# Splitting the token axis of a projection's products as 512 and 128 instead of 320 and 320

## What is computed

```python
def conformer_conv_branch(glu_in, conv_buf, w_dw, b_dw, ln_g, ln_b, w_pw):
    u = glu_in[..., :D_CONV] * jax.nn.sigmoid(glu_in[..., D_CONV:])
    v, new_buf = causal_depthwise_conv(u, conv_buf, w_dw, b_dw)
    v = jax.nn.silu(layer_norm(v, ln_g, ln_b))
    return v @ w_pw, new_buf
...
        gates = jax.nn.sigmoid(gate_logits.astype(jnp.float32))
        g_a, g_b = gates[..., :D_MODEL], gates[..., D_MODEL:]
        merged = (g_a * y_a.astype(jnp.float32) + g_b * y_b.astype(jnp.float32)).astype(x.dtype)
        x = x + merged @ p['w_out'][l]
```

## Time and profile before

| | us |
|---|---|
| time, median of 2 runs | 1771.34 |
| the two runs | 1770.57, 1772.12 |
| profiled execution: span, first to last instruction | 1769.8 |
| profiled execution: its own whole time | not listed apart; the two runs are 0.8 and 2.3 above its span |
| TensorE busy in the span | 1729.8 (98%) |
| VectorE busy | 1282.0 (72%) |
| ScalarE busy | 873.9 (49%) |
| mean granted TensorE clock | 0.995 of full speed |

### The profile page before, as it was taken

One profiled execution on the slowest core, in us unless ns is written; L12 is line 12 of the kernel. 1 busy time (PEld: TensorE's weight loads), 2 busy tenths in 40 slices (PEclk: granted clock), 3 DMA queues, 4 the chain that ended last, 5 costly groups with the idle time before them and its releaser, 6 DMA issues.

```text
span 1769.8 us, 29064 instructions
## 1 busy us (share of the span) xinstructions
PE 1729.8 (98%) x11823; PEld 1685.3 (95%) x11823; DVE 1282.0 (72%) x1630; ACT 873.9 (49%) x1491; POOL 116.5 (7%) x173
## 2 busy tenths in 40 slices
PE   7999999999999999999999999999999999999997
PEld 7999999999988999899899989999999999999997
DVE  6864783575757989889898987875547936863865
ACT  5431442243588567747756772274335423431443
POOL 0000000000011011030222102000100000000000
PEclk9999999999999999999999999999999999999998
DMA  4222212213253255183446517212422222212212
GB/s 165 84 72 96 75 69 84 107 49 122 81 172 93 77 168 139 59 227 119 108 126 178 155 49 184 84 61 83 139 84 84 72 69 99 86 61 94 96 63 69
DMA packets 54324, 181.50 MB, mean 103 GB/s; under 512 B 7312, under 2 KB 9520, under 8 KB 49840
## 3 DMA queue, kind: packets, MB, share of 16 engines
q1 hardware_dynamic: 40176, 137.41, 23.7%
q0 software_dynamic: 14016, 42.24, 9.1%
HBM read 155.56 MB, written 16.20 MB: 97 GB/s over the span
## 4 chain that ended last, share of the span: by engine, by line
PE 80%; DVE 11%; ACT 4%; issue 3%; DMA 1%; DVEq 0%; ACTq 0%; SPq 0%
PE ps L1754 30%; PE ps L1862 23%; PE ps L1762 15%; PE ps L1779 4%; PE ps L1815 2%; DVE w_lo L1069 1%; DVE v L1467 1%; DVE acc L1081 1%; PE ps L1797 1%; PE ps L2000 1%; PE ps L1987 1%; ACT w_hi L559 1%; DVE z L1565 1%; DVE y L1616 1%; PE ps L1994 1%
## 5 line engine op out<-in xcount | busy, mean ns | idle before, releaser
L1754 PE MATMUL ps<-xa_hi,w_hi 128*128 128x320 f32 x1328 | 312.9, 317 | 0.1
L1754 PE MATMUL ps<-xa_lo,w_hi 128*128 128x320 f32 x1328 | 302.8, 309 | 0.0
L1862 PE MATMUL ps<-t_hi,w_hi 128*128 128x320 f32 x952 | 295.3, 310 | 6.6 <-DVE sq L1136 5.4
L559 ACT CAST w_hi<-w_raw 128x1024 fp32r<-128x1024 f32 (+2 forms) x183 | 174.6, 955 | 252.2 <-PE ps L1762 174.1
L1862 PE MATMUL ps<-t_hi,w_lo 128*128 128x320 f32 x952 | 294.8, 310 | 0.0
L1862 PE MATMUL ps<-t_lo,w_hi 128*128 128x320 f32 x952 | 294.8, 310 | 0.0
L1069 DVE TENSOR_TENSOR w_lo<-w_raw,w_hi 128x1024 fp32r<-128x1024 f32 (+2 forms) x183 | 203.4, 1112 | 91.5 <-ACT w_hi L559 84.2
L1754 PEld LDWEIGHTS ps<-xa_hi,w_hi 128*128 128x128 f32 x1328 | 222.3, 188 | 12.2 <-issue 10.6
L1467 DVE SCALAR_TENSOR_TENSOR v<-ext_a,par,v 128x640 f32<-128x640 f32 x240 | 211.5, 881 | 15.3 <-ACT v L791 5.8
L1754 PEld LDWEIGHTS ps<-xa_lo,w_hi 128*128 128x128 f32 x1328 | 222.6, 188 | 0.0
L1762 PE MATMUL ps<-xa_hi,w_lo 128*128 128x320 f32 x1328 | 211.7, 310 | 0.0
(11 more groups left out here) (329 smaller groups left out, 2995.5 us busy)
## 6 DMA issues: line engine op xcount, KB each, us to landing
w_raw<-in_w_mix SPq DMA_DIRECT2D x56, 512.0 KB, 3.8
raw_b<-in_w_sp SPq DMA_DIRECT2D x18, 1024.0 KB, 5.0
w_raw<-in_w_sp SPq DMA_DIRECT2D x16, 1024.0 KB, 4.8
w_raw<-in_w_down SPq DMA_DIRECT2D x32, 512.0 KB, 3.7
w_raw<-in_w_tail SPq DMA_DIRECT2D x32, 512.0 KB, 3.7
w_raw<-in_w_gu SPq DMA_DIRECT2D x20, 512.0 KB, 3.8
acb<-cum_dram POOLq DMA_DIRECT2D x20, 512.0 KB, 6.6
w_raw<-in_w_ssm SPq DMA_DIRECT2D x32, 256.0 KB, 2.9
```

What stands on the lines that cost most here:

```text
L559: nc.scalar.copy(hi, w_raw[:, b, 0:width]).then_inc(hi_done, 1)
L1754: nc.tensor.matmul(psj[:, b, u, 0:TH], hi[:, cols], act_in[:, k, u * TH:(u + 1) * TH], start=(k == 0 and n == 0), stop=False)
L1862: last = nc.tensor.matmul(ps[:, sp_set(n) + BANK[q], 0:TH], w[:, k * P:(k + 1) * P], t[:, X_OF[q], k * TH:(k + 1) * TH], start=(first and ...
```

## The change

The jobs of the output projection go through a new function, `job_by_splits`. It cuts the 640 tokens at 512: one product takes tokens 0 to 511, the other 512 to 639. The accumulator of a job is the same pair of banks, now read as one run of 1024 floats of which the first 640 are used: the first product fills the first bank, the second one takes 128 floats of the second. VectorE reads the run of 640 in one piece (`run_out`), where it read two of 320. All 8 jobs run by parts, the first too: it waits for the hi weights at its start, for `ln_lo` ahead of each chunk, and for the lo weights only behind the eighth chunk.

```diff
+        def run_out(b):
+            return psj[:, b].rearrange("p u n -> p (u n)")[:, 0:T]
...
-                nc.vector.tensor_tensor(halved(prod[:]), job_out(b), halved(gate_a[:, c]), ALU.mult).then_inc(evac_done[b], 1)
+                nc.vector.tensor_tensor(prod[:], run_out(b), gate_a[:, c], ALU.mult).then_inc(evac_done[b], 1)
...
+            def job_by_splits(half, b, chunks, in_hi, in_lo, before=None):
+
+                pe.wait_ge(hi_done, 2 * half + b + 1)
+                pe.wait_ge(evac_done[b], half + 1)
+                hi, lo = job_weights(half, b)
+                out = psj[:, b].rearrange("p u n -> p (u n)")
+                parts = (slice(0, 512), slice(512, T))
+                for k in range(chunks):
+                    if before:
+                        before(k)
+                    cols = slice(k * P, (k + 1) * P)
+                    for n, act_in in enumerate((in_hi, in_lo)):
+                        for part in parts:
+                            nc.tensor.matmul(out[:, part], hi[:, cols], act_in[:, k, part],
+                                             start=(k == 0 and n == 0), stop=False)
+                pe.wait_ge(lo_done, 2 * half + b + 3)
+                for k in range(chunks):
+                    cols = slice(k * P, (k + 1) * P)
+                    for part in parts:
+                        last = nc.tensor.matmul(out[:, part], lo[:, cols], in_hi[:, k, part],
+                                                start=False, stop=(k == chunks - 1))
+                last.then_inc(job_done, 1)
...
-            job(half, 0, KM, ln_hi, ln_lo, lambda k: pe.wait_ge(xlo_ready, S_LN + k + 1))
-            job(half, 1, KM, ln_hi, ln_lo)
+            job_by_splits(half, 0, KM, ln_hi, ln_lo, lambda k: pe.wait_ge(xlo_ready, S_LN + k + 1))
+            job_by_splits(half, 1, KM, ln_hi, ln_lo)
             for j in range(1, KM // 2):
                 for b in range(2):
-                    job(half + j, b, KM, ln_hi, ln_lo)
+                    job_by_splits(half + j, b, KM, ln_hi, ln_lo)
```

## The result

The changed kernel takes 1782.99 us (median of two runs, 1781.98 and 1784.01) against 1771.34, 11.6 us slower. The ratio on record is 1.0061, interval 1.0042 to 1.0079 (the two medians alone give 1.0066). In a later comparison with more runs (5 of the changed kernel, 17 of the one before) it took 1782.63 against 1771.68, a ratio of 1.0062, interval 1.0050 to 1.0074. The profiled execution took 1784.01, with a span of 1782.0.

What follows compares the result with a forecast made beforehand. The prediction took PE to bound the kernel, busy 98% of the span. Later jobs +7.6 and first job +1.6 us gave +9.2: span 1769.8 to 1779.0, plus 1.5 for the median, 1780.5 us; range 1774 to 1803.

Steps and rivals of the forecast that it cites:

- The pair: Output projection on PE: one long plus one short product take 338.7 ns, 45.3 more than before; chance 0.69.
- The value taken from products of 64 columns of another data type: Weight load of 112 ns, read from plain f32 products with 128x128 weights, taken as the short product's time.
- 53 (load hidden): Short product's lower bound, 53.3 ns of columns alone; rival with loads hidden, both forms, chance 0.10.
- 227 (plain f32 rate): Short product's upper bound, 226.7 ns at a quarter rate; rival total +29.8 us, 1801, chance 0.18.
- the 13.4 ns: Time per 320-column product beyond its 133.3 ns of columns; taken as fixed, giving the long product 226.7 ns.
- its other candidate: Long product's extra time goes with the columns: 234.7 ns, pair 346.7, total +10.6 us (1781.9).
- The Trainium skill's price: Sustained 81 ns per 128-column and 131 per 512-column product, loads included; 192 pairs would save 15.6 us (1755.7).
- Seven later jobs: Projection jobs after the first, 24 pairs each: 168 x 45.3 ns = +7.6 us, all on the path.
- The first job: Projection's first job: a 1.61 us stall goes, a 2.29 us wait for lo input comes; ends 1.57 us later.
- What was to cost nothing: Accumulator read as one run of 640 (0.824 us either way), weight loads and splits, work of DVE, ScalarE and queues.
- The pair that would make the kernel 2% slower: Pair of some 490 ns (185 ns more), or a new stall, needed for over 2% slower; chance 0.03.
- the clock falling behind a wait of 2.3 us: Half clock after the first job's lo-input wait, 1.6 us lost; given a third, outside the sum.

Runs made afterwards that it cites:

- long products with half loads: Changed kernel, but the 512-token products load 64 weight columns instead of 128, save the first and last of each accumulation; 1771.56 us in one run.
- 448 and 192: Changed kernel with the tokens cut at 448 instead of 512, the accumulator run beginning 64 floats later; 1775.94 us, ratio 1.0025.
- 384 and 256: Changed kernel with the tokens cut at 384 instead of 512, the accumulator run beginning 128 floats later; 1772.30 us, ratio 1.0004.
- the order alone: Kernel before with 320 and 320 tokens kept, only the projection's first job going by parts; 1773.93 us against 1771.47, ratio 1.0013.
- the split alone: Changed kernel with its first job chunk by chunk behind the lo weights, as before the change; 1780.68 us against 1771.47, ratio 1.0053.

## Why the prediction was right

**The pair.** Predicted 338.7 ns, measured 340, by the mechanism that was predicted: the short product lasts as long as the load for the next long one. That the two agree to 1 ns is in part luck, because the two terms were off in opposite directions: 112 and 226.7 predicted, 109 and 231 by the starts of the loads. These starts, to the ns (medians over the seven later jobs), give the time of a product of every width that was run:

| columns | where | measured, ns | columns at 2.4 GHz + 13.4 | columns x 146.7 / 320 |
|---|---|---|---|---|
| 128, next load halved | long products with half loads | 57 | 66.7 | 58.7 |
| 128 | changed kernel | 109 | 66.7 | 58.7 |
| 192 | 448 and 192 | 108 | 93.4 | 88.0 |
| 256 | 384 and 256 | 117 | 120.1 | 117.3 |
| 320 | kernel before | 147 | 146.7 | 146.7 |
| 384 | 384 and 256 | 176 | 173.4 | 176.0 |
| 448 | 448 and 192 | 205 | 200.1 | 205.3 |
| 512 | changed kernel | 231 | 226.7 | 234.7 |

The load's time, 108 to 109 ns, holds behind 128 and 192 columns; a product of 256 columns takes longer by itself and hides it. The value taken from products of 64 columns of another data type carried over to within 4 ns. Of the bounds for the short product, 53 (load hidden) and 227 (plain f32 rate) are both far off.

The prediction took the 13.4 ns as a fixed price per product, and this choice is not borne out: from 128 to 448 columns the times without a wait go with the columns to within 2 ns (last column of the table), which was its other candidate (234.7 for the long product). At 512 columns the measured 231 lies between the two, and why it does is not shown.

**The Trainium skill's price** of 81 and 131 ns ("TensorE: Matmul & The Clock Gate", section "Back-to-back issue gap") gave a pair of 212 ns and a faster kernel. The measured pair is 340 ns, so the trace decides against it for products of this type, each with a load of its own.

**Seven later jobs.** Predicted +7.6 us, measured +7.84: 168 x 46.6 ns.

**The first job.** Predicted +1.57, measured +1.71; the wait predicted 2.29, measured 2.20 us. Of this, the order costs some 1.1 us, by the differences given with the run of the order alone.

**What was to cost nothing** cost nothing: the read of the accumulator stands at 825 ns, and VectorE's and ScalarE's busy time is as before.

**What else was off.** Nothing here carried the sum. I said that products' starts would alternate by some 227 and 112 ns; it is the loads' starts that do, while those of the products lie 280 and 60 ns apart. The pair that would make the kernel 2% slower was given as some 490 ns; 293.4 + 185 is 478. And I gave a third to the clock falling behind a wait of 2.3 us: at 2.2 us it fell in none of three profiles, while behind the 2.5 to 2.8 us of four other kernels it fell in all four.

**What stays open.** Predicted were 1780.5 us, +9.2, and the stretch has 9.55; the time moved by 11.0 to 11.6. In the two profiled executions the spans differ by 12.2: 1.08 ahead of the stretch, 9.55 in it, and 1.6 behind it. The last part has a cause that shows: after the second wait of the kind of the earlier trace rows the changed kernel's first profile has half clock, which the profile of before has not.

```profile
1410.00:1415.00 5.00, 3.86 (x16) 3.89 (x17) 4.11 (x8) 0.67 (x2) 0.00 (x0) 0.66 0.09 16
```

The changed kernel's second profile settles more. Ahead of its last ten us it has half clock in two places, at 98 us and at 1408, as the profile of before has at 98 and at 528; the first profile of the changed kernel has three. First before, then the second profile:

```profile
528.00:532.00 4.00, 3.85 (x11) 2.85 (x12) 0.40 (x1) 1.94 (x4) 0.00 (x0) 0.57 0.58 191
...
1408.00:1412.00 4.00, 3.65 (x14) 3.68 (x15) 2.99 (x6) 0.10 (x1) 0.00 (x0) 0.57 0.06 9
```

With as many falls in either, the spans are 1769.8 and 1779.3 us: 9.5 apart, as much as the stretch. So in this pair nothing is left beyond the stretch, and what the medians have beyond it is most likely falls elsewhere. The mean granted clock of the runs points the same way: all seven of the changed kernel have 0.995 or 0.996, while of the 17 of the kernel before eight have 0.997 or 0.998 (1769.3 to 1771.6 us) and nine 0.994 or 0.995 (1771.7 to 1775.2). Whether the change makes falls elsewhere likelier, or that is chance, no run here tells.

## What to carry to other kernels

When one operand load goes with every product, price a product as the larger of its own time and the load of the next one: here 128 weight columns need some 109 ns, which 256 columns of input cover (117 ns) and 192 do not (an estimated 88, at the rate of 320 columns). A cut of the same work into a large and a small product is therefore not neutral; an even cut is, or any cut whose small part still covers a load. And before moving a product forward in the order, look at which input it will wait for next: here a wait of 1.6 us became one of 2.2.

## What the runs showed that was not expected

The granted clock falls to half around short waits, each time for some 3.4 us at a price of some 1.6, and not reliably: behind 1.6 us in one kernel (the split alone) and not in another (the one before), behind none of three waits of 2.2, and behind all four of 2.5 to 2.8 us in the first job. The two waits of 2.68 us of the earlier trace rows stand in all ten profiles, and at 8 of these 20 the clock fell, shortly before the wait ended or within some 1.4 us after it. A wait is not needed either: in the changed kernel's first profile the clock is 0.50 from 504 to 506 us, where PE has no idle time listed since 495, but from 499.0 to 503.4 us only products of 32 and 128 columns.

Timed runs of one and the same kernel lie between 1769.3 and 1775.2 us, so a change of 1 or 2 us is read from its stretch of the trace and not from the time.
